# Attention of two transformer layers on one core: a head's value products as one batch in column halves

## What is computed

```python
s = jnp.einsum('bnikgd,bnukd->bkgniu', qb, kband).astype(jnp.float32) * (D ** -0.5)
s = s - slopes * dist; s = jnp.where(allowed, s, NEG_INF)
p = jax.nn.softmax(jnp.concatenate([s, sink_col], axis=-1), axis=-1)[..., :-1]
o = jnp.einsum('bkgniu,bnukd->bnikgd', p.astype(v.dtype), vband)
```

## Time and profile before

| | |
|---|---|
| median of 3 runs | 1996.39 us (1995.15 to 1996.77) |
| the profiled execution | 1996.64 us |
| its span, first to last instruction | 1994.9 us |
| mean granted TensorE clock | 0.998 |
| PE busy | 1970.6 us (99%) |
| DVE busy | 1092.7 us (55%) |
| ACT busy | 853.5 us (43%) |
| POOL busy | 201.4 us (10%) |
| value products (L2812), both layers | 560 records, 919.8 to 1568.2 us |

### The profile page before, as it was taken

One profiled execution on the slowest core, in us unless ns is written; L12 is line 12 of the kernel. 1 busy time (PEld: TensorE's weight loads), 2 busy tenths in 40 slices (PEclk: granted clock), 3 DMA queues, 4 the chain that ended last, 5 costly groups with the idle time before them and its releaser, 6 DMA issues.

```text
span 1994.9 us, 31378 instructions
## 1 busy us (share of the span) xinstructions
PE 1970.6 (99%) x11631; PEld 1727.1 (87%) x11631; DVE 1092.7 (55%) x1878; ACT 853.5 (43%) x1274; POOL 201.4 (10%) x195
## 2 busy tenths in 40 slices
PE   8999999999999999999999999999999999999998
PEld 7989989999888988889988888888889888888887
DVE  6235999555653566577654433444656654433443
ACT  6224665543223554466643222234666543212333
POOL 2004111200100110001001100110014001100100
PEclk9999999999999999999999999999999999999999
DMA  4322111233333324331033332332332133323332
GB/s 140 110 83 78 53 54 54 78 92 95 90 102 107 95 84 115 107 96 42 12 95 95 99 102 84 95 110 79 103 87 65 43 95 95 108 82 95 95 101 79
DMA packets 320578, 174.21 MB, mean 87 GB/s; under 512 B 5216, under 2 KB 317920, under 8 KB 320496
## 3 DMA queue, kind: packets, MB, share of 16 engines
q1 hardware_dynamic: 320496, 173.11, 29.7%
HBM read 170.99 MB, written 2.10 MB: 87 GB/s over the span
## 4 chain that ended last, share of the span: by engine, by line
PE 95%; DVE 3%; issue 1%; ACT 1%; DMA 0%; SPq 0%; POOL 0%; POOLq 0%; DVEq 0%; ACTq 0%
PE ps L2194 54%; PE ps L2200 27%; PE ps L2812 3%; PE ps L2772 2%; PE ps L2797 2%; PE ps L2347 1%; PE ps L2408 1%; PE ps L2750 1%; PE ps L2751 1%; PE ps L2687 1%; PE ps L2441 0%; DVE w_lo L1385 0%; PE ps L2822 0%; DMA x_rows<-x 0%; PE ps L2299 0%
## 5 line engine op out<-in xcount | busy, mean ns | idle before, releaser
L2194 PE MATMUL ps<-z_hi,w_hi 128*128 128x512 f32 (+2 forms) x2032 | 623.6, 345 | 0.0
L1385 DVE TENSOR_TENSOR w_lo<-raw,w_hi 128x1024 fp32r<-128x1024 f32 (+2 forms) x298 | 385.9, 1295 | 430.3 <-ACT w_hi L829 429.0
L2194 PE MATMUL ps<-z_lo,w_hi 128*128 128x512 f32 (+2 forms) x2032 | 614.8, 341 | 0.0
L829 ACT ACTIVATE w_hi<-raw 128x1024 fp32r<-128x1024 f32 (+2 forms) x298 | 328.3, 1102 | 443.1 <-PE ps L2200 408.0
L2200 PE MATMUL ps<-z_hi,w_lo 128*128 128x512 f32 (+2 forms) x2032 | 433.0, 341 | 0.0
L2194 PEld LDWEIGHTS ps<-z_hi,w_hi 128*128 128x128 f32 x2032 | 352.0, 189 | 50.9 <-issue 3.1
L2194 PEld LDWEIGHTS ps<-z_lo,w_hi 128*128 128x128 f32 x2032 | 350.8, 189 | 44.7
L2200 PEld LDWEIGHTS ps<-z_hi,w_lo 128*128 128x128 f32 x2032 | 333.3, 189 | 45.2
L2194 PE MATMUL ps<-g_hi,w_hi 128*128 128x512 f32 (+1 forms) x539 | 209.4, 390 | 0.0
L2194 PE MATMUL ps<-g_lo,w_hi 128*128 128x512 f32 (+1 forms) x539 | 208.8, 389 | 0.0
L760 POOL TENSOR_TENSOR g_lo<-gv,g_hi 128x512 f32 x65 | 84.4, 1299 | 1062.5 <-ACT g_hi L1240 1062.5
(11 more groups left out here) (352 smaller groups left out, 2413.3 us busy)
## 6 DMA issues: line engine op xcount, KB each, us to landing
raw<-w_gate_up SPq DMA_DIRECT2D x88, 512.0 KB, 3.9
raw<-w_down SPq DMA_DIRECT2D x48, 704.0 KB, 4.8
raw<-w_in SPq DMA_DIRECT2D x44, 512.0 KB, 3.9
raw<-w_up SPq DMA_DIRECT2D x44, 512.0 KB, 3.8
raw<-w_out SPq DMA_DIRECT2D x24, 512.0 KB, 4.0
raw<-w_in_b SPq DMA_DIRECT2D x14, 512.0 KB, 3.8
raw<-w_in_a SPq DMA_DIRECT2D x12, 512.0 KB, 3.8
raw<-w_branch SPq DMA_DIRECT2D x8, 512.0 KB, 3.9
```

What stands on the lines that cost most here:

```text
L829: act.activation(w_hi[s][:, 0:width], raw[s][:, 0:width], ACT.Copy).then_inc(hi_done, 1)
L1385: dve.tensor_tensor(w_lo[s][:, 0:width], raw[s][:, 0:width], w_hi[s][:, 0:width].bitcast(F32), ALU.subtract).then_inc(lo_done, 1)
L2194: pe.matmul(out, w_hi[s][:, w0 + k * P:w0 + (k + 1) * P], rhs[:, lo:lo + width], start=a, stop=False)
```

## The change

The value products of a head are issued together, in step n for head n - 3 behind the scores of block 1, once all four blocks are copied. Each turned block has a buffer of its own, two sets of four in turn by the head's number. Each product is issued as two, for columns 0 to 63 and 64 to 127 of the turned block, writing the two halves of the output's partitions. The semaphore `y` counts heads and not blocks. VectorE takes block 1 and waits for the scores of block 2 before it normalises.

```diff
-        pts = [sb(at, f"pts{i}", [P, 3 * P]) for i in range(2)]
+        pts = [[sb(at, f"pts{i}_{b}", [P, blocks * P]) for b, blocks in enumerate((2, 3, 3, 2))] for i in range(2)]
...
@@ ScalarE: copy (VectorE's copy of block 3 alike)
-                    act.wait_ge(*s.at("y", 4 * h + (b - 1)))
-                    act.activation(pts[b % 2][:, 0:width], ps[3][:, b % 2, 0:width], ACT.Copy).then_inc(s["pa"], 1)
+                    act.wait_ge(*s.at("y", h - 1))
+                    act.activation(pts[h % 2][b][:, 0:width], ps[3][:, b % 2, 0:width], ACT.Copy).then_inc(s["pa"], 1)
...
@@ VectorE: step
                         summed(h, r, 0)
                         scored(h, 1)
+                        summed(h, r, 1)
+                        scored(h, 2)
                     if done:
...
-                        dve.wait_ge(*s.at("y", 4 * h - 8))
+                        dve.wait_ge(*s.at("y", h - 2))
...
                     if front:
-                        summed(h, r, 1)
-                        scored(h, 2)
                         dve.memset(carrier[:, :], 0.0)
...
@@ TensorE
+            def column_halves(out, weights, moving, start, stop):
+
+                for t in range(2):
+                    x = pe.matmul(out[t * VD:(t + 1) * VD], weights[:, t * VD:(t + 1) * VD], moving, start=start, stop=stop)
+                return x
...
+                def values(h, r, memory, kv, n_):
+                    pe.wait_ge(*s.at("out", h - 2))
+                    pe.wait_ge(*s.at("pa", 3 * h + 3))
+                    pe.wait_ge(*s.at("pd", h + 1))
+                    for b in range(4):
+                        _, width = span(memory, b, l)
+                        for j in range(width // P):
...
+                            x = column_halves(y_bank(r)[:, b * VS:(b + 1) * VS], pts[h % 2][b][:, j * P:(j + 1) * P], v,
+                                              j == 0, j == width // P - 1)
                     x.then_inc(s["y"], 1)
...
-                        if b == 0 and n_ >= 3:
-                            values(h - 3, r, n_ - 3 >= QH, 3, last_kv, n_ - 3)
-                        elif b and back:
-                            if (n_, b) == (2, 1):
+                        if b == 1 and n_ >= 3:
+                            if n_ == 3:
                                 pe.wait_ge(*s.at("va", (1, 2)[l]))
-                            values(h - 2, rb, memory, b - 1, back_kv, n_ - 2)
+                            values(h - 3, r, n_ - 3 >= QH, last_kv, n_ - 3)
```

More of the change, by code:

```diff
@@ L377, in build @@
         att_counts = {"mk_hi": 1, "mk_lo": 1, "scaled": 10, "q_hi": 10, "q_lo": 10, "va": 1, "vd": 1, "v23": 1, "s": 4 * AH, "ls": 4 * AH, "neg": AH, "exp": 4 * AH, "t": 4 * AH,
-                      "pa": 3 * AH, "pd": AH, "y": 4 * AH, "sum": QH, "inv": AH, "out": AH, "bias": QH,
+                      "pa": 3 * AH, "pd": AH, "y": AH, "sum": QH, "inv": AH, "out": AH, "bias": QH,
                       "turned": KD, "hi": KD, "lo": KD}
@@ L2071, in copy @@
                     dve.wait_ge(*s.at("t", 4 * h + (b + 1)))
-                    dve.wait_ge(*s.at("y", 4 * h + (b - 1)))
-                    dve.tensor_copy(pts[1][:, 0:width], ps[3][:, 1, 0:width]).then_inc(s["pd"], 1)
+                    dve.wait_ge(*s.at("y", h - 1))
+                    dve.tensor_copy(pts[h % 2][b][:, 0:width], ps[3][:, 1, 0:width]).then_inc(s["pd"], 1)
                 def negated(h, r):
@@ L2799, in turn @@
                     x.then_inc(s["t"], 1)
[L2801 to L2813, removed]
+                def values(h, r, memory, kv, n_):
[5 more added lines that the diff above has]
+                        for j in range(width // P):
+                            block = key_block(memory, b, j, l)
+                            if memory:
+                                v = mv[:, 2 * l + block, (n_ - QH) * VS:(n_ - QH + 1) * VS]
+                            else:
+                                v = v_tok[:, block, kv * VS:(kv + 1) * VS]
+                            x = column_halves(y_bank(r)[:, b * VS:(b + 1) * VS], pts[h % 2][b][:, j * P:(j + 1) * P], v,
+                                              j == 0, j == width // P - 1)
                     x.then_inc(s["y"], 1)
@@ L2827, in step @@
                     front, back = n_ < AH, 2 <= n_ < AH + 2
-                    kv, back_kv, last_kv = (h, h - 2, h - 3) if l else (g, g - 1 if r < 2 else g, g - 1)
+                    kv, last_kv = (h, h - 3) if l else (g, g - 1)
                     rb, memory = (r + 1) % 3, n_ - 2 >= QH
```

## The result

| | before | after |
|---|---|---|
| median of 6 runs each | 1995.83 us (1995.15 to 1996.77) | 2009.28 us (2009.01 to 2012.24) |
| the profiled execution | 1996.64 us | 2009.33 us |
| its span | 1994.9 us | 2007.5 us |
| mean granted TensorE clock | 0.998 | 0.998 |
| PE busy | 1970.6 us | 1963.5 us |

The ratio is 1.007, with a 95% interval of 1.0057 to 1.0083: the changed kernel is slower, and the forecast of 2008.7 us was 0.6 us off. The two medians differ by 13.45 us, where 12.3 were forecast. The last two lines of the table are differences of starts: 918.65 to 985.30 and 918.40 to 991.79 in layer 0, 1512.66 to 1569.58 and 1519.14 to 1582.27 in layer 1. They add up to 12.9 us, so all of the 12.6 us by which the span grew is lost there.

A forecast was written before the change was run, and what follows sets the result against it. The prediction took the kernel as a queue of TensorE matmuls (95% of the chain). A longer ring adds +7.0 us in layer 0 and +5.3 in layer 1, +12.3 on the 1996.39 us median: 2008.7 us, range 2003 to 2017.

The forecast's parts named there:

- The ring: Attention, turn of block 1 to next head's, through VectorE's copy of block 3: 4.86 us in layer 0, 3.84 in layer 1.
- The batch: A head's value products on TensorE, issued together: 1.53 us in layer 0 (2.00 before), 1.29 in layer 1 (1.56 before).
- the change of mode: TensorE going between whole and half columns, in and out once a batch: 0.35 us together; range took 0.15 to 0.65.
- The sum: Both layers' attention: 13 steps each, layer 0 +4.95 and +2.0 us, layer 1 +5.3, ends nothing, together +12.3 us.
- the first step: Start of each layer's attention: the batch leaves this step, -1.5 us in layer 0 and -1.3 in layer 1.
- the prediction's "nothing" at the ends: Each layer's attention: batch leaves the first step (-1.5, -1.3 us), stands alone behind the last (+1.5, +1.3).
- the ring doesn't bind: Rival, attention: queues run at their own work, 3.95 us and 3.16 a head, -9.7 us, 1986.7 us; chance 0.08.
- TensorE's own sum of 3.84: Layer-0 head: what TensorE alone would need with the batch, 3.84 us; 3.16 in layer 1.
- The 3.95 us that the prediction gave VectorE: Layer-0 head: VectorE's need, the 4.31 us interval less its one idle gap of 0.36 us.
- the changes of mode cost nothing: Rival, TensorE's batch: ring binds but shorter by about 0.4 us, as TensorE waits anyhow; +3.2 us, 1999.6; chance 0.08.
- the halves don't overlap: Rival, value products: batch takes 2.35 and 1.91 us, 22.2 us on top, +34.5, 2030.9 us; chance 0.04.
- The rule of the Trainium skill: Value products: column tiling needs a free dimension of at most 64 to help; products would stay at 2.00 and 1.56 us.

## Why the prediction was right

**The ring.** It was right as a mechanism and nearly so in each term. In the rows of after, layer 0: the turn and scores of block 1 take 0.70 us (0.69 forecast), the batch 1.46 (1.53), turn and scores of block 2 0.86 (0.85), the step to VectorE 0.03 (0.04), normalising 0.76 (0.75), block 2 0.48 (0.48), the copy 0.42 (0.42), and from there to the turn 0.14 (0.10). The sum is 4.85 for 4.86. (The rows give 1.41 for the batch and 0.91 behind it; the 0.05 us of the way back that show in the turn are counted with the batch.) In layer 1 it is 3.86 for 3.84. The idle before the turn was put at 1.0 and 0.7 us: the distance from the end of the scores of block 3 to that turn is 931.63 - 930.62 = 1.01 and 1538.58 - 1537.90 = 0.68, of which the profile puts 0.87 and 0.54 down to the copy. That the ring caused the loss, and was not merely there, is shown by cutting it in two ways: in VectorE's order (back to 1996.27 us) and at the bank (2001.35 us).

**The batch.** 40 records of 64 columns run from 927.58 to a last start 1164 ns later, on average 29.8 ns apart; forecast were 29 to 30. The mis-sized term is the change of mode: 0.35 us taken, 0.29 measured in two layers with four batches a head. The single records of the change tell which half of it. Going in, the first pair starts 0.10 us late and the second 0.05: 0.15 in all, for 0.14 forecast, though no row stood behind 0.05 of that. Coming out, the turn starts 0.10 us late and its second record 0.05: 0.15, for 0.21. It made the batch 0.07 us too long in the sum, which the longer step from the copy to the turn and some hundredths elsewhere made up. The agreement to 0.01 us is partly luck, and the range's 0.15 to 0.65 for this term held.

**The sum.** The ring was forecast at 12.3 us in all and the medians differ by 13.45. That the forecast is only 0.6 us off is luck in part: it was added to 1996.39 us, and the kernel before has a median of 1995.83 over its six runs. Layer 0 was put at +7.0 us and came to +6.7, layer 1 at +5.3 and came to +6.2. Added up from one turn of block 1 to the next, the time of after less that of before (in layer 0 the 13 steps are nine banded ones and four others):

| us | layer 0 | layer 1 |
|---|---|---|
| the first step, which has no batch | -1.4 (-1.5 forecast) | -0.5 (-1.3) |
| the 13 steps with a batch and new scores | +4.9 and +2.2 (+4.95 and +2.0) | +5.7 (+5.3) |
| behind them, to the output matmuls | +1.0 (+1.5) | +1.0 (+1.3) |

The term that was furthest off is the first step of layer 1. The batch has left it, yet it became only 0.5 us shorter. TensorE idles there for a score bank, and VectorE, which is to free that bank, waits for the bias that GpSimd adds up. Timeline of PE, then of DVE, the change:

```profile
1521.87 0.44 PE L2803 MATMUL ps<-con,ls 128*128 128x128 f32 x2 [0.66 <-DVE row_max L2056]
```

```profile
1521.38 0.42 DVE L2056 CUSTOM_DVE_ANT_0 ls<-ps,bias 128x256 f32<-128x256 f32 x1 [0.80 <-POOL bias L803]
```

So the prediction's "nothing" at the ends was -0.3 us in layer 0 and +0.5 in layer 1, which nearly cancel. The 13 steps of layer 1 came to 5.7 us since they took 3.42 us each before and 3.85 after, where the forecast had 3.43 and 3.84.

**The rivals.** That the ring doesn't bind is excluded by the 0.87 us of idle. What its opening would bring is shown by the batch behind the last scores. Layer 0 then runs at 3.86 us, TensorE's own sum of 3.84. The 3.95 us that the prediction gave VectorE was too high: its one idle row was taken off the interval, but waits too short to be rows were left in, and its busy time is 3.70. The rival's price of 9.7 us was not reached: the steady steps bring 9 x 0.45 + 13 x 0.09 = 5.2 us, and of these 3.6 are left in the whole. In layer 1 a head takes 3.34 us where TensorE's sum is 3.16. The rest lies ahead of the turn of block 3: it starts at 1541.26, about 0.19 us later than its place behind the scores would be and 0.14 us after the end of ScalarE's copy of block 1 (1541.11), the same 0.14 us as behind VectorE's copy in the change. Why ScalarE comes no sooner was not followed up.

That the changes of mode cost nothing behind the idle is excluded too. The batch lies in the ring, ahead of the wait, and a longer batch lengthens the interval one for one (0.72 us more of batch with whole columns, 0.72 us more of interval).

That the halves don't overlap is excluded by 29.8 ns a record, and more plainly by the single records, which the timeline merges: the two of a pair start 7 ns apart and the next pair 58 ns after them. A whole record in a batch takes 2.18 / 20 = 109 ns.

The rule of the Trainium skill that spoke against the change, in TensorEngine Tiling (Array Packing), section Performance Considerations, is not borne out to the letter: neither free dimension is 64 or less here (128 and 65), and the halves still save 0.72 us of 2.18. But 65 is only one over the limit, and the first block of the kernel before shows that the gain does hang on the short side. There half columns stand beside 128 moving elements. Timeline of PE, before:

```profile
209.50 0.39 PE L2457 MATMUL ps<-qe,st 128*64 128x128 f32 x4
209.72 0.39 PE L2455 MATMUL ps<-sc,vh 128*64 128x128 f32 x4
```

Four records, two pairs, take 0.22 us: 109 ns a pair, as much as one record of the turns, whole columns with 128 moving elements (109 ns as well). So halves with 128 moving elements save nothing, with 65 they save nearly half. Lengths between were not measured.

A reason that fits the whole record is the weight load: a record takes 109 ns with 65 moving elements and 109 with 128, so the moving elements don't set its pace. The whole record's load is 192 ns long in the records and the half's 138. The Trainium skill, TensorE: Matmul & The Clock Gate, section LDWEIGHTS (loading the stationary operand), gives the load as the columns divided by 1.2, in ns, which makes an estimate of 107 for 128 columns and 53 for 64. The trace's 109 and 58 ns lie close to it, as they would if the load set the pace and the two halves loaded side by side. For the halves the moving elements do count, as 58 ns at 65 against 109 at 128 show. What sets the pace of either is argued from these rows and not shown by an experiment.

## What to carry to other kernels

Moving work on the critical engine is also moving it between a neighbour's two waits: write down each chain from a buffer's write to its next write, across all engines, and add up its rows before and after; the engine's own total (here 0.5 us a head less in layer 0) says nothing when such a ring is longer. If an in-order engine takes a result that comes behind the moved work, put first what frees the buffer and last what nobody needs yet: here two or three instructions a head placed behind a copy were worth 13 us. A tiling mode that costs a fixed price to enter and leave is to be batched, and batch and mode are to be measured each alone: here either one alone loses 14 us or more against the kernel before, and both together gain 3.5 us (by the ratio, 0.15% with an interval of 0.06 to 0.24%) when the batch stands behind the last scores.

## What the runs showed of the hardware

**Half columns with a short moving operand.** Two records on 64 columns each, with 65 moving elements in fp32, take 58 ns together; one on 128 columns takes 109. (A float32 product is two such records, so a whole product takes 218 ns and its two halves 117.) With 128 moving elements a pair of half records takes 109 ns too, and the gain is gone.

**The price of the mode.** 0.29 us there and back, in a layer with batches of 8 and 12 half records and in one with batches of 8.

**A small VectorE instruction beside GpSimd.** The one that makes `neg_max` from two SBUF operands of four elements takes 0.16 us alone in layer 1, and 0.63 to 0.65 where it starts during one of GpSimd's additions of 128x256. Its form in layer 0 takes 0.22 us alone, and beside a 0.83 us addition it ends with that addition. Timelines of DVE and POOL, the change, layer 0:

```profile
927.00 0.89 DVE L2078 SCALAR_TENSOR_TENSOR neg_max<-row_max,par,minus 128x4 f32<-128x4 f32 x1
```

```profile
927.05 0.83 POOL L795 TENSOR_TENSOR bias<-att_con,con 128x384 f32<-128x384 f32 x1 [4.11 <-DVE row_max L2056]
```

In one execution it took 3.06 us beside a run of additions of 10.37 / 15 = 0.69 us each. The Trainium skill, SBUF — State Buffer, section SBUF: two separate sides, says that a GpSimd instruction which reads SBUF and a VectorE instruction with two SBUF inputs share a pair of ports, that the one which starts first holds it for its whole instruction, and that the other waits. The 0.89 beside 0.83 us agrees that one waits out the other, but not on who goes first: by the records VectorE's instruction starts 0.05 us earlier and yet ends last. (The profile's spans on GpSimd are rough.) The 3.06 us do not fit a wait for one instruction: it started during one addition and lasted over four more, to the end of their run. That came once in the ten traces, cost TensorE 2.18 us of idle, and was followed by 3.4 us at the lower clock; why the wait went past the end of an addition is open.
